# Down weights with four consecutive rows per partition, gate and up columns read with a stride of four

## What is computed

```python
D_MODEL = 1024; N_EXPERTS = 32; D_EXPERT = 512
...
"w_exp_gate": nrm((DEPTH, N_EXPERTS, D_MODEL, D_EXPERT), D_MODEL ** -0.5),
"w_exp_up": nrm((DEPTH, N_EXPERTS, D_MODEL, D_EXPERT), D_MODEL ** -0.5),
"w_exp_down": nrm((DEPTH, N_EXPERTS, D_EXPERT, D_MODEL), D_EXPERT ** -0.5),
...
for e in range(N_EXPERTS):
    a = jax.nn.silu(x @ w_g[e]) * (x @ w_u[e])
    y = y + gate[:, e:e + 1] * (a @ w_d[e]).astype(jnp.float32)
```

## Time and profile before

| | |
|---|---|
| median of 3 runs | 1016.0 us (1014.78 to 1016.91) |
| profiled execution: its own time | 1009.28 us |
| its span in the trace | 1007.4 us |
| PE busy | 854.1 us (85% of the span) |
| DVE, ACT, POOL busy | 209.0, 145.5, 123.7 us |
| mean TensorE clock granted | 0.888 of full speed |
| weight transfers of experts | 96 of 2048 KB each |
| all packets of DMA | 70782, 261.26 MB |
| chain that ended last | PE 57%, DMA 35%, DVE 3% |

### The profile page before, as it was taken

How to read it: one execution, slowest core, us unless ns; L and a number is a source line. 1 busy time by engine, 2 the same in 40 slices (tenths; PEclk the granted TensorE clock), 3 DMA queues, 4 the chain that set the end, 5 groups by cost and what they waited for, 6 DMA issues and landing times.

```text
span 1007.4 us, 11776 instructions
## 1 busy us (share of the span) xinstructions
PE 854.1 (85%) x4620; PEld 499.7 (50%) x4620; DVE 209.0 (21%) x559; ACT 145.5 (14%) x357; POOL 123.7 (12%) x223
## 2 busy tenths in 40 slices
PE   6998999999989999998688878878787887887860
PEld 4656666745664466554344444444444444444430
DVE  2004442006531301533110101101010110110104
ACT  3103231102351111330000000000000000000001
POOL 2101000001010000013211111111111111111113
PEclk9997555996559999989799999999999999999995
DMA  9948911223020234142399999999999999999925
GB/s 235 362 166 309 324 47 42 84 84 136 1 82 3 98 152 155 54 157 84 134 411 400 424 404 409 410 396 417 384 417 405 413 422 411 421 417 409 424 116 156
DMA packets 70782, 261.26 MB, mean 259 GB/s; under 512 B 13239, under 2 KB 29647, under 8 KB 62144
## 3 DMA queue, kind: packets, MB, share of 16 engines
q1 hardware_dynamic: 62416, 244.57, 62.7%
q0 software_dynamic: 8192, 16.27, 4.6%
q10 hardware_dynamic: 144, 0.00, 0.0%
HBM read 249.37 MB, written 24.97 MB: 272 GB/s over the span
## 4 chain that ended last, share of the span: by engine, by line
PE 57%; DMA 35%; DVE 3%; issue 2%; SPq 1%; POOL 1%; ACT 1%; ACTq 0%; POOLq 0%; DVEq 0%
DMA ring<-in_w_exp_up 32%; PE pA L907 12%; PE pA L900 10%; PE pA L1178 7%; PE pS L1198 6%; PE pS L940 6%; PE pA L974 5%; PE pTr L955 3%; PE pTr L1167 2%; PE pTr L891 1%; SPq L454 1%; PE pS L944 1%; DMA srow<-slot_d 1%; DMA zone<-y_d,slot 1%; PE pA L1127 1%
## 5 line engine op out<-in xcount | busy, mean ns | idle before, releaser
L1178 PE MATMUL pA<-ring,zone 128*64 128x256 f32 x2048 | 248.3, 398 | 86.7 <-DMA ring<-in_w_exp_up 55.1
L1178 PEld LDWEIGHTS pA<-ring,zone 128*64 128x64 f32 x2048 | 152.7, 143 | 175.4 <-DMA ring<-in_w_exp_up 68.3
L1198 PE MATMUL pS<-ring,zone 128*64 128x512 f32 x512 | 116.9, 599 | 0.5 <-DVE zone L1511 0.5
L907 PE MATMUL pA<-ring,hT 128*128 128x512 f32 (+1 forms) x240 | 106.3, 601 | 1.0 <-DVE hT L1264 1.0
L900 PE MATMUL pA<-hT,ring 128*128 128x320 f32 x320 | 89.3, 442 | 0.5 <-DVE hT L1264 0.5
L1500 DVE TENSOR_TENSOR zone<-zone,pA 128x256 f32<-128x256 f32 x32 | 13.5, 421 | 337.6 <-ACT zone L813 337.6
L900 PEld LDWEIGHTS pA<-hT,ring 128*128 128x128 f32 x320 | 62.1, 195 | 26.6 <-issue 1.8
L907 PEld LDWEIGHTS pA<-ring,hT 128*128 128x128 f32 (+1 forms) x240 | 41.3, 175 | 61.4 <-issue 60.9
L940 PE MATMUL pS<-zone 64*128 64x128 f32 (+3 forms) x128 | 66.4, 634 | 2.5 <-issue 2.5
L1198 PEld LDWEIGHTS pS<-ring,zone 128*64 128x64 f32 x512 | 33.9, 137 | 57.7 <-issue 54.8
L813 ACT ACTIVATE zone<-pA 128x256 f32<-128x256 f32 x32 | 12.3, 383 | 329.9 <-PE pA L1178 329.9
(11 more groups left out here) (201 smaller groups left out, 606.3 us busy)
## 6 DMA issues: line engine op xcount, KB each, us to landing
ring<-in_w_exp_gate SPq DMA_DIRECT2D x32, 2048.0 KB, 16.4
ring<-in_w_exp_up SPq DMA_DIRECT2D x32, 2048.0 KB, 21.3
ring<-in_w_exp_down SPq DMA_DIRECT2D x32, 2048.0 KB, 12.2
ring<-in_w_in SPq DMA_DIRECT2D x6, 2048.0 KB, 21.6
y_d<-cmask SPq DMA_DIRECT2D x1, 8192.0 KB, 41.8
ring<-in_w_out SPq DMA_DIRECT2D x2, 2048.0 KB, 18.2
ring<-in_w_ck SPq DMA_DIRECT2D x1, 2048.0 KB, 25.1
ring<-in_w_cv SPq DMA_DIRECT2D x1, 2048.0 KB, 7.5
```

The costliest lines, as they stand in the source:

```text
L907: last = mm(bank[0:rows, 0:512], lhs(c), w[:, c, cols_], start=c == 0, stop=c == k - 1)
L1178: last = mm(pA[b][half * SLOTS:(half + 1) * SLOTS, x * HF:(x + 1) * HF], xeT[:, b, c, :], w[:, c, half * HF:(half + 1) * HF], start=c == 0 ...
L1198: last = mm(pS[b][half * SLOTS:(half + 1) * SLOTS, 0:512], aT[:, b, f % 2, (f // 2) * SLOTS:(f // 2 + 1) * SLOTS], w[:, f, half * 512:(hal ...
```

## The change

Down weights are loaded as `(p c) n`: partition `q` holds the consecutive rows `4q` to `4q + 3`, so a partition's part is one run of 16 KB in HBM. The row in partition `q` and block `f = 2 h + k` is now `4 q + 2 h + k`. For this the gate and up matmuls read other columns of their weights: half `h` reads, for `k` of 0 and 1 in turn, the 128 columns `4 q + 2 h + k`, a stride of four float32, where it read 256 neighbouring columns. The result columns are dense as before, so everything behind them (activation, `turn_act`, `down`) has the same instructions and the same addresses.

```diff
@@ expert_weights
                 if n < 2:
                     dst, src = by_k(s), src.rearrange("(p c) n -> p c n", c=C)
                 else:
-                    dst, src = by_k(s, FC), src.rearrange("(c p) n -> p c n", p=P)
+                    dst, src = by_k(s, FC), src.rearrange("(p c) n -> p c n", c=FC)
                 sp.dma_start(dst, src).then_inc(w_in_s[s], 16)
@@ gate_up
                         for half in range(2):
                             last = mm(pA[b][half * SLOTS:(half + 1) * SLOTS, x * HF:(x + 1) * HF], xeT[:, b, c, :],
-                                      w[:, c, half * HF:(half + 1) * HF], start=c == 0, stop=c == C - 1)
+                                      w[:, c, :].rearrange("p (q h k) -> p h k q", h=2, k=2)[:, half, :, :], start=c == 0, stop=c == C - 1)
                     last.then_inc(up_read if x else gate_read, 1)
```

## The result

The changed kernel takes 1138.2 us (median of 4 runs, 1136.83 to 1139.02) against 1015.5 us for the kernel before (median of 4 runs, 1014.78 to 1016.91; three of them gave the 1016.0 of the table ahead); the ratio is 1.120, 95% interval 1.117 to 1.123. It is slower by 122.7 us. The forecast was 1009.1 us, with a range from 1002 to 1020. The rival in which the stride halves the moving stream was priced at 1141 us and had a chance of 0.17; that is what happened.

The account below looks back on a forecast made before the run. DMA, streaming expert weights, was taken as the bound. Longer down runs save 6.9 us and the strided read costs nothing, so 1016.0 - 6.9 = 1009.1 us, with a range from 1002 to 1020.

Parts of the forecast that it names:

- The rival in which the stride halves the moving stream: Gate and up matmuls: L1178 doubles, PE needs 19.7 us per expert, about 1141 us; chance 0.17.
- What bounds the kernel: Expert loop: DMA is full at 410 GB/s, 15.79 us per expert; PE needs 12.39, so 3.4 us are free.
- The transfers: Down weights: 16 KB instead of 4 KB runs save 0.24 us per transfer, 6.9 us over 29.
- The strided read: Gate and up matmuls: the stride costs 0.3 us of PE per expert against 3.4 us free, so nothing.
- The sum of the rival: Doubled gate and up: 114 us over 29 experts, 8 for expert 1, 3.7 for the last; about 1141 us, chance 0.17.
- The added-cost rival: Gate and up: 0.36 ns added per column, 10.6 us per expert, PE level with DMA; 1012 to 1019 us, chance 0.08.
- the rival without gain: Down transfers: packet size doesn't move the ceiling of the rate; 1014 to 1018 us, chance 0.12.
- a factor of 1.43: Gate and up matmuls: slowdown from which PE, instead of DMA, becomes the bound.

Follow-up runs that it names:

- gate_only: Against the kernel before: only gate read with the stride of four, up dense, down weights in runs of 4 KB; 1023.6 us, ratio 1.0068.
- pairs: Against the changed kernel: neighbouring columns 4q+2h and 4q+2h+1 read one after the other, activation turn reads every second column; 1011.0 us, ratio 0.9945 to the kernel before.
- stride_two: Against the kernel before: half h of gate and up reads columns 2j + h, a stride of 8 bytes; 1015.5 us (one run).
- front_strided: Against the kernel before: only the L907 matmuls with eight blocks, in the front, read their 512 moving columns with a stride of four; 1124.9 us (one run).
- one_half_strided: Against the kernel before: the first half of gate and up reads its 256 columns with a stride of four, the second dense; 1140.4 us (one run).

## Why the prediction was wrong

**What bounds the kernel: right.** DMA was the bound, and 3.4 us of PE were free per expert. `gate_only` used 3.6 and lost 7 us in all, so PE is just past the edge there.

**The transfers: right, somewhat smaller.** 6.9 us were predicted; the layout alone gave 5.5 us (3.4 to 7.7) and with the pairs 5.6. The rate in the loop rose from 410 to 413 and 414 GB/s. The period was said to go from 15.79 to between 15.5 and 15.6 us. Counted as the prediction counts, over the 27 intervals from the second down issue, it is (942.15 - 520.13) / 27 = 15.63 us with the pairs, 0.16 us less where 0.24 were predicted; over all 29 intervals it goes from 15.64 to 15.50. One trace can't size so small a term: in `stride_two`, with down in runs of 4 KB and DMA as the bound, the same count gives (945.70 - 516.38) / 27 = 15.90. So the 5.5 us rest on the times. The 2.5 us that the prediction worked out as an estimate from the Trainium skill, DMA: Bandwidth & Descriptors, section Why small descriptors are slow, lie under the interval.

**The strided read: wrong, and this is the step that failed.** The prediction said "A float32 matmul already takes its columns at the pace at which strided ones can be read. Read as a lowest time per column, the stride costs 0.03 ns of 0.82". The lowest time was taken from loads of the stationary operand, 0.85 ns a column. A moving float32 stream takes 1.74 ns for a column alone in its line in the halves, and 1.76 in a full-width matmul (`front_strided`); with that, gate and up took 14.6 us per expert: the stride costs 7.3 us of PE, where the sum had 0.3, and 3.4 were free. The idea of a lowest time was right, its size was off by a factor of two, and the unit is the line, not the column.

The row was also the wrong witness. In `pairs` the loads of L1186 have a stride of 8 bytes, two touches on a line, and take 206 ns against 142 for the same group in the kernel before (row below), hardly different from the 200 at 32 bytes.

```profile
L1186 PEld LDWEIGHTS pS<-ident,zone 128*128 128x128 f32 x64 | 6.5, 142 | 25.3 <-issue 25.2
```

Loads slow down at both steps that were seen, 8 and 32 bytes; moving columns hardly slow down at 8. The load rows thus say nothing of how a moving stream counts lines, and that 0.85 lay near 0.82 was no sign of a common limit. I took the value of the sum from them because their stride is longer, and gave the doubling 0.17 although the rule of the Trainium skill, Advanced Engine Details and Errata, section Memory Cachelines, spoke for it.

**The sum of the rival: right, in part by luck.** It named two ways to a doubling. A limit for both halves together falls with `one_half_strided` and `front_strided`; that a single float32 stream slows down is what the runs show. It had 3.9 us per expert over 29 experts, 114 us in all, plus 8 for expert 1 and 3.7 for the last, 125.7 together against 122.7 between the medians. Measured: period 19.54 against 15.64 us, 3.9 x 29 = 113 us. The prediction had 19.7 and 15.79, both some 0.15 too long, so that the difference came out. The first and last starts of L1178 (behind the durations; the kernel before, then the changed one) give the rest:

```profile
L1178 PE MATMUL pA<-ring,zone x2048: 378/379/689, 469.3 to 964.9; 128*64 128x256 f32 x187
```

```profile
L1178 PE MATMUL pA<-ring,zone x2048: 629/629/693, 475.6 to 1093.8; 128*64 128x256 f32 x187
```

From the first to the last it is 618.2 us instead of 495.6, 122.6 more, so 9.6 belong to the first and last experts, for which the prediction had 11.7. The spans differ by more, 1137.2 - 1007.4 = 129.8, and 6.3 of that come before the first gate matmul, where nothing was changed. The other runs that leave the front as it was begin it between 469.3 and 477.2 us. Why the front varies so stays open, and an early start doesn't by itself make the 1007.4 us of before: `stride_two` also begins at 469.3 and has a span of 1013.7.

**The added-cost rival and the rival without gain** are both excluded: L1178 took 2.0 times as long, not 1.44, and the layout alone has a gain whose interval leaves out zero.

**The range** left out the one case on the other side of a factor of 1.43. The prediction had found that factor, and had found that no row showed a strided moving operand; a price with no row that can double the busiest engine's work deserved a range that reached it.

## To carry to other kernels

When a layout is changed so that a transfer becomes longer, look at which engine then walks with a step through the tile: here 5.5 us of DMA time were bought with 3.9 us per expert of TensorE. If a float32 matmul must read its moving operand with a step, order the reads so that each 16-byte line is touched twice in a row; then it costs 5% of the stream instead of 100%, and the step can be undone where the result is small. Before pricing a read by another operand's row, measure that read alone; the front of the kernel offers a place for it.

## What the runs showed of the hardware

A moving float32 stream pays 1.73 to 1.74 ns per 16-byte line at steps of 8, 12 and 16 bytes, and 0.83 ns per column when dense (two streams side by side; one alone takes 1.76 and 0.84 ns per column at 16 and 4 bytes). Two matmuls in the two column halves of the array, one strided and one dense, both go at the strided one's pace. Loads of 128 float32 columns for a transpose take 206 ns at a step of 8 bytes, 200 at 32 and 142 dense. At a step of 32 bytes the moving stream is 2% slower than at 16, for which I have no cause.
